# One stream of modulation units through a fourteen-sublayer network on one core: its joins moved into output projections, squares moved from VectorE to ScalarE

## The chip, the cores and the metric

One core of a Trainium2 chip runs the whole program. The metric is the device time of one execution in microseconds (us); the median of several runs is given with the lowest and the highest. One further execution was profiled, and its time stands beside the span that the trace covers. Engines are named as in the profile: PE (TensorE), PEld (its weight loads), DVE (VectorE), ACT (ScalarE), POOL (GpSimd) and SP (SyncE).

## The reference, cut to what matters

Two networks follow each other on the same 256 tokens of width 1024. The first has two layers of three sublayers, the second four layers of two. Each sublayer normalises `x`, scales and shifts it by modulation vectors, computes a mixer or a feed-forward part, and adds the result to `x` through a gate:

```python
mod = (c_act @ mod_w[layer] + mod_b[layer]).reshape(B, N_SUB, 3, D_MODEL)
h, g = sublayer_input(x, norm_g[layer, 0], mod[:, 0])     # rmsnorm(x)*(1+scale)+shift, 1+gate
x = x + MACARON_W * g * swiglu(h, ffn_w_gu[layer, 0], ffn_w_down[layer, 0])
...
mod = c_act @ ada_w[i] + ada_b[i]                          # second network: 6 vectors a layer
h = _rmsnorm(x, norm_g[i, 2]) * (1.0 + sc_f[:, None]) + sh_f[:, None]
y = jnp.square(jax.nn.relu(h @ w1)) @ w2
x = x + gt_f[:, None] * _rmsnorm(y, norm_g[i, 3])
```

The modulation needs a 1024 x 3072 matrix times one vector for each sublayer. It depends on `c` alone, so it can be computed at any time before its sublayer begins.

## The kernel before

The fourteen sublayers, numbered 0 to 13, are ffn1, sb, ffn1, ffn1, lru, ffn1, mla, ffn2, conv, ffn2, pool, ffn2, mla, ffn2. Here ffn1 is the gated feed-forward part, sb the stick-breaking attention, lru the recurrence, mla the second network's attention and ffn2 its squared-ReLU feed-forward part. Products are made in fp32 from a high and a low part of both operands, three matmuls each (L1274 to L1276 with 512 columns, L1375 to L1377 with 256).

**Weights.** SP's queue brings the weights in chunks of 1 MB into `raw` (4 buffers). A chunk is two pieces. For each piece ACT makes `w_hi` (L836) and DVE makes `w_lo` (L1761) in `pieces(a, b)`, and PE uses it in `piece`. There are 4 slots for pieces (`OPS`), so piece p can be made only when PE has used piece p-4. An ffn1 has 11 gate-up jobs of 4 pieces and a down projection of two jobs of 11; an ffn2 has 8 gate-up jobs of 4 pieces and a down projection of two jobs of 16.

**Modulation units.** Each sublayer's modulation is a group of 16 units (`UNITS`). POOL's queue brings a unit's 768 KB into one half of `mod_raw` (`mod_half`, L617 to L621), when the unit two earlier has been used. DVE multiplies it by its entry of `c` and adds it to `mod_acc` (`mod_add`, L1782). Two folds (`mod_fold`, L1788) reduce the accumulator to `mod_t`, PE joins it by 8 small matmuls (`mod_sum`, L1423 to L1428, which waits for both folds), and DVE adds the bias into `mv` (`mod_finish`, L1796). `GROUPS` gives each ffn1 two groups, sb, mla and ffn2 one, until group 13 is given out, so that groups fall on sublayers 0, 1, 2, 3, 5, 6, 7, 9 and 11. The last group of each of these nine is "late": its `mod_sum` is the first thing that PE does in the next sublayer, and its `mod_finish` stands in `a_values`, once the tokens are normalised.

**The boundary of two sublayers.** After the last piece (`last_piece`) DVE multiplies the output by the gate and adds it to `x` (`first_half` and `second_half`, L1882), ACT and DVE normalise, and PE transposes the tokens (`turn_x`, L1319). Where no group is late, PE fills some of this time with small dummy matmuls (`keep_busy`, L1308) before the turn.

**ffn2 gate-up.** ACT makes ReLU into `sig`, DVE squares it into `ev` (L2022), ACT copies it to `hid_hi` and POOL subtracts to `hid_lo` (`hid_low`, L658). Each engine has its own program, in order; semaphores join them.

## Time and profile before

| | before |
|---|---|
| median of 3 runs | 2348.78 us (2347.01 to 2350.11) |
| the profiled execution | 2343.05 us, of which the trace spans 2341.4 us |
| mean granted TensorE clock | 0.958 of full speed |
| PE busy | 2106.8 us (90% of the span) |
| PEld busy | 1906.4 us (81%) |
| DVE busy | 1647.2 us (70%) |
| ACT busy | 1196.4 us (51%) |
| POOL busy | 356.4 us (15%) |
| HBM read | 530.12 MB, 227 GB/s over the span |

All times of the trace are microseconds from the start of its span. Busy shares are means over stages with different limits. A window's PEclk is the share of full TensorE speed that was granted in it; its DMA share is the mean busy share of the core's 16 DMA engines.

### The profile page before, as it was taken

What the parts mean: (1) busy time and instruction counts of PE and PEld (TensorE: products, weight loads), DVE (VectorE), ACT (ScalarE), POOL (GpSimd) and SP (SyncE); (2) the same over time, 40 slices, a digit from 0 to 9 for tenths busy, and PEclk for the clock granted to TensorE, in tenths of its full rate; (3) what the DMA queues carried; (4) which work ended last, traced back from release to release, by engine and by line L of the source; (5) the groups of instructions that cost most, each with busy time, mean ns of one, the idle gap of its engine ahead of it and who ended that gap; (6) DMA issues with size and microseconds to landing.
All of it is one profiled execution on the core that took longest, in us unless ns stands there. A gap on an engine that the chain in (4) does not pass through costs nothing.

```text
span 2341.4 us, 36873 instructions
## 1 busy us (share of the span) xinstructions
PE 2106.8 (90%) x14192; PEld 1906.4 (81%) x14192; DVE 1647.2 (70%) x1861; ACT 1196.4 (51%) x1836; POOL 356.4 (15%) x548
## 2 busy tenths in 40 slices
PE   1999998999899896999887999889997899898998
PEld 1998886998798794998775998758985898777987
DVE  7787865787777867776887776536767776764654
ACT  2553556544554465553565544536544554575543
POOL 2121100111121002121000220430211121000210
PEclk8999999999999997999998999899998899999999
DMA  9798883898888963798666677643777378442653
GB/s 330 259 320 302 281 303 109 284 320 296 269 309 289 284 217 73 257 313 300 212 236 171 222 280 265 180 115 119 266 285 229 103 249 292 143 138 72 196 191 107
DMA packets 298483, 537.72 MB, mean 230 GB/s; under 512 B 11487, under 2 KB 188434, under 8 KB 298352
## 3 DMA queue, kind: packets, MB, share of 16 engines
q1 hardware_dynamic: 262048, 356.55, 46.9%
q0 software_dynamic: 36032, 178.33, 21.8%
q8 instruction: 88, 1.44, 0.2%
q10 hardware_dynamic: 272, 1.05, 0.1%
q14 instruction: 43, 0.35, 0.0%
HBM read 530.12 MB, written 1.11 MB: 227 GB/s over the span
## 4 chain that ended last, share of the span: by engine, by line
PE 73%; DVE 13%; ACT 5%; issue 4%; DMA 3%; POOL 1%; DVEq 0%; ACTq 0%; POOLq 0%
PE bk L1375 12%; PE bk L1377 12%; PE bk L1376 12%; PE bk L1276 7%; PE bk L1275 7%; PE bk L1274 7%; DVE mod_acc L1782 3%; DVE w_lo L1761 3%; DMA mod_raw<-in_ada_w 2%; ACT w_hi L836 2%; PE bk L1262 1%; PE bk L1264 1%; PE bk L1263 1%; PE bk L1319 1%; PE bk L1636 1%
## 5 line engine op out<-in xcount | busy, mean ns | idle before, releaser
L1761 DVE TENSOR_TENSOR w_lo<-raw,w_hi 128x1024 fp32r<-128x1024 f32 (+5 forms) x720 | 832.6, 1185 | 486.7 <-ACT w_hi L836 484.9
L836 ACT ACTIVATE w_hi<-raw 128x1024 fp32r<-128x1024 f32 (+5 forms) x720 | 684.7, 978 | 637.2 <-PE bk L1276 341.9
L1375 PE MATMUL bk<-a_hi,w_hi 128*128 128x256 f32 x2332 | 665.3, 285 | 19.7 <-DVE mv L1799 10.0
L1377 PE MATMUL bk<-a_hi,w_lo 128*128 128x256 f32 x2332 | 663.6, 285 | 0.0
L1376 PE MATMUL bk<-a_lo,w_hi 128*128 128x256 f32 x2332 | 663.5, 285 | 0.0
L1375 PEld LDWEIGHTS bk<-a_hi,w_hi 128*128 128x128 f32 x2332 | 451.5, 194 | 22.3 <-DVE mv L1799 10.8
L1376 PEld LDWEIGHTS bk<-a_lo,w_hi 128*128 128x128 f32 x2332 | 451.5, 194 | 0.0
L1377 PEld LDWEIGHTS bk<-a_hi,w_lo 128*128 128x128 f32 x2332 | 451.4, 194 | 0.0
L1782 DVE SCALAR_TENSOR_TENSOR mod_acc<-mod_raw,cact,mod_acc 128x1536 f32<-128x1536 f32 x182 | 329.8, 1812 | 29.8 <-DMA mod_raw<-in_ada_w 18.3
L1276 PE MATMUL bk<-w_hi,hid_lo 128*128 128x512 f32 x832 | 327.9, 394 | 0.0
L1274 PE MATMUL bk<-w_hi,hid_hi 128*128 128x512 f32 x832 | 324.5, 390 | 3.3 <-DVE w_lo L1761 3.2
L1275 PE MATMUL bk<-w_lo,hid_hi 128*128 128x512 f32 x832 | 326.6, 393 | 0.0
L658 POOL TENSOR_TENSOR hid_lo<-ev,hid_hi 128x512 f32 (+1 forms) x108 | 139.7, 1305 | 546.8 <-ACT hid_hi L1013 440.3
L1274 PEld LDWEIGHTS bk<-w_hi,hid_hi 128*128 128x128 f32 x832 | 156.6, 188 | 39.2 <-issue 4.9
L1275 PEld LDWEIGHTS bk<-w_lo,hid_hi 128*128 128x128 f32 x832 | 156.6, 188 | 35.7
L1276 PEld LDWEIGHTS bk<-w_hi,hid_lo 128*128 128x128 f32 x832 | 156.8, 188 | 31.9
L621 POOL DMA_DIRECT2D mod_raw<-in_ada_w x128 | 69.2, 541 | 632.8 <-DVE mod_acc L1782 518.8
L621 POOL DMA_DIRECT2D mod_raw<-in_mod_w x80 | 43.3, 541 | 432.2 <-DVE mod_acc L1782 323.7
L1319 PE MATMUL bk<-ident,tmp 128*128 128x128 f32 x224 | 47.5, 388 | 60.5 <-DVE tmp L1834 60.2
L1140 ACT ACTIVATE hid_hi<-ev 128x512 f32 (+1 forms) x44 | 27.9, 633 | 139.3 <-DVE ev L2232 139.3
L1274 PE MATMUL bk<-w_hi,a_hi 128*128 128x512 f32 x176 | 71.6, 407 | 28.6 <-POOL a_lo L813 21.7
L1319 PEld LDWEIGHTS bk<-ident,tmp 128*128 128x128 f32 x224 | 39.7, 204 | 66.5 <-DVE tmp L1834 66.3
(361 smaller groups left out, 2997.1 us busy)
## 6 DMA issues: line engine op xcount, KB each, us to landing
raw<-in_ffn_w SPq DMA_DIRECT2D x128, 1024.0 KB, 5.6
mod_raw<-in_ada_w POOLq DMA_DIRECT2D x128, 768.0 KB, 6.2
raw<-in_ffn_w_gu SPq DMA_DIRECT2D x88, 1024.0 KB, 7.4
mod_raw<-in_mod_w POOLq DMA_DIRECT2D x80, 768.0 KB, 6.9
raw<-in_ffn_w_down SPq DMA_DIRECT2D x40, 1024.0 KB, 7.3
first_mod<-in_mod_w SPq DMA_DIRECT2D x16, 768.0 KB, 13.0
raw<-in_sb_w_qkv SPq DMA_DIRECT2D x12, 1024.0 KB, 9.1
raw<-in_conv_w_pw SPq DMA_DIRECT2D x12, 1024.0 KB, 6.2
```

What stands on the lines that cost most here:

```text
L621: pool.dma_start(mod_raw[:, h, :].unsqueeze(1), w.rearrange("(k p) m -> p k m", p=P)[:, bass.ds(r, 1), at + h * MODW:at + (h + 1) * MODW]) ...
L658: pool.tensor_tensor(hid_lo[:, tiles(pair, width), :], ev[:, slot, :, :], hid_hi[:, tiles(pair, width), :].bitcast(F32), ALU.subtract).the ...
L836: ins = act.activation(o(w_hi[:, p % OPS, :]), r(raw[:, c % RAWS, :]), ACT.Copy)
L1274: pe.matmul(o, xh[:, s], wh, start=first, stop=False)
L1275: pe.matmul(o, xh[:, s], wl, start=False, stop=False)
L1276: ins = pe.matmul(o, xl[:, s], wh, start=False, stop=last)
L1319: ins = pe.transpose(turned_x(w, j)[:, P * b:P * b + P], xt[:, b, P * j:P * j + P], ident[:, :])
L1375: pe.matmul(o, wh, a_hi[:, f, :], start=(f == 0), stop=False)
L1376: pe.matmul(o, wh, a_lo[:, f, :], start=False, stop=False)
L1377: ins = pe.matmul(o, wl, a_hi[:, f, :], start=False, stop=(f == KD - 1))
L1761: ins = dve.tensor_tensor(o(w_lo[:, p % OPS, :]), r(raw[:, c % RAWS, :]), o(w_hi[:, p % OPS, :].bitcast(F32)), ALU.subtract)
L1782: dve.scalar_tensor_tensor(out=a, in0=src, scalar=cc[:, bass.ds(r, 1)], in1=a, op0=ALU.mult, op1=ALU.add).then_inc(mod_used, 1)
```

## The change

The units become one stream of 208 that `STREAM` deals to the sublayers: 24, 16, 16, 24, 0, 24, 12, 28, 0, 32, 0, 24, 8, 0. A group may now begin in one sublayer and end in a later one. Sublayers 7 and 9 (ffn2) take 28 and 32 units instead of 16, mla takes 12 and 8 instead of 16 and 0, ffn1 24 or 16 instead of 32. The convolution has none, as before.

`JOINS` names for each sublayer the group joined in the middle and the one joined at its end. In ffn1 the middle join stays in gate-up job 9. The other joins go into `job`, after piece number `at` of an output projection, and their `mod_finish` stands among the pieces there. No join is left at a boundary, so each boundary has `turned()` and `keep_busy`. `mod_sum` writes another bank and its wait for a free bank is left to the caller.

Fold 0 follows the last unit of its group at once; fold 1 (`last_fold`) follows the next piece or pieces. In ffn2's gate-up each job takes two units (before, one), and `DOWN` lists after which pieces of the down projection a unit follows: for 28 units after every second piece, for 32 after two of three. The square of the ReLU goes from DVE (16 in each ffn2) to ACT. DVE's and POOL's loops over jobs of ffn1 and ffn2 are written out.

```diff
-        GROUPS = {"ffn1": 2, "sb": 1, "mla": 1, "ffn2": 1}
-        stages, c, w, hid, grp = [], 0, 0, 0, 1
+        STREAM = (24, 16, 16, 24, 0, 24, 12, 28, 0, 32, 0, 24, 8, 0)
+        JOINS = {0: (1, None), 1: (2, None), 2: (3, None), 3: (4, 5), 5: (6, None), 6: (7, None), 7: (8, 9), 9: (10, 11), 11: (12, None), 12: (13, None)}
+        DOWN = {24: (1, 4, 7, 10, 13, 17, 20, 23), 28: (0, 2, 4, 6, 8, 10, 12, 16, 18, 20, 22, 24), 32: (0, 1, 3, 4, 6, 7, 9, 10, 12, 13, 16, 17, 19, 20, 22, 23)}
...
         for n, kind in enumerate(kinds):
-            groups = list(range(grp, min(grp + GROUPS.get(kind, 0), len(kinds))))
-            late = stages[-1]["groups"][-1] if n and stages[-1]["groups"] else None
-            stages.append(dict(kind=kind, n=n, c=c, w=w, hid=hid, groups=groups, late=late, nth=kinds[:n].count(kind)))
-            c, w, hid, grp = c + CHUNKS[kind], w + WJOBS[kind], hid + PAIRS.get(kind, 0), grp + len(groups)
+            mid, end = JOINS.get(n, (None, None))
+            stages.append(dict(kind=kind, n=n, c=c, w=w, hid=hid, units=STREAM[n], mid=mid, end=end,
+                               nth=kinds[:n].count(kind)))
+            c, w, hid = c + CHUNKS[kind], w + WJOBS[kind], hid + PAIRS.get(kind, 0)
...
         def mod_out(w):
-            return bk[:, 4 * (w % 2) + 1, S:S + MODC // P]
+            return bk[:, 4 * (w % 2) + 3, 0:MODC // P]
...
+            def loads(n):
+                for _ in range(n):
+                    s = k.next("load")
+                    if s < NSTREAM:
+                        mod_half(1 + s // UNITS, s % UNITS // 2, s % 2)
...
                 if st["kind"] == "ffn2":
-                    g, n = st["groups"], st["hid"]
-                    def two_low(i, b):
+                    n = st["hid"]
+                    for j in range(8):
+                        loads(min(2, st["units"]))
                         for e in range(2):
-                            hid_low(n + 4 * i + 2 * b + e, 4 * i + 2 * b + e, e)
-                    with pool.Fori(0, 4) as i:
-                        for b in range(2):
-                            two_low(i, b)
-                            if g and b == 1:
-                                mod_load(g[0], i + 1)
+                            hid_low(n + 2 * j + e, 2 * j + e, e)
                     gate_tile(st["n"])
-                    if g:
-                        for r in range(5, KD):
-                            mod_next(g[0], r)
-                    if g:
-                        mod_next(g[0], KD)
+                    loads(max(0, st["units"] - UNITS))
...
                 elif st["kind"] == "ffn1":
-                    g, n = st["groups"][0], st["hid"]
-                    mod_rest(g, lambda i, b: hid_low(n + 2 * i + b, 2 * i + b, b))
-                    for b in range(3):
-                        if b:
-                            mod_next(g + 1, b)
-                        hid_low(n + 8 + b, 8 + b, b % 2)
+                    n, more = st["hid"], st["units"] > UNITS
+                    for b in range(11):
+                        loads(2 if b < 8 else more)
+                        hid_low(n + b, b, b % 2)
                     gate_tile(st["n"])
...
+                    n, s0 = st["hid"], 16 * st["nth"]
                     with act.Fori(0, 4) as i:
                         for b in range(2):
                             pieces(p + 4 + 4 * b, p + 8 + 4 * b, i)
                             for e in range(2):
                                 relu(w + b, c + 2 * b, i, e)
                             for e in range(2):
-                                if e:
-                                    is_read(act, w + b, i)
-                                else:
-                                    act.wait_ge(prod_ready, 8 * st["nth"] + 2 * i + b + 1)
+                                act.wait_ge(sig_ready, n + 2 * b + e + 1 + 4 * i)
+                                act.wait_ge(hid_ready, n + 2 * b + e + 1 + 4 * i)
+                                act.activation(ev[:, e, :, :], sig[:, e, :, :], ACT.Square).then_inc(prod_ready, 1)
+                            act.sem_inc(bank_free[(w + b) % 2], 1)
+                            for e in range(2):
+                                act.wait_ge(prod_ready, s0 + 2 * b + e + 1 + 4 * i)
                                 act.activation(hid_hi[:, tiles(4 * i + 2 * b + e), :], ev[:, e, :, :], ACT.Copy)\
                                     .then_inc(hhi_ready, 1)
...
-            def job(c, w, i, xs, kt0, kts, ready, outs=None, tail=None):
+            def job(c, w, i, xs, kt0, kts, ready, outs=None, tail=None, join=None, at=None):
                 is_free(pe, w, i)
                 n = (kts + 1) // 2
                 for q in range(n if tail is None else n - 1):
                     piece(2 * c + q, i, ready, xs, kt0 + 2 * q, outs or by_feature(w), q == 0, q == n - 1)
+                    if join is not None and q == at:
+                        mod_sum(join, w)
...
             def mod_sum(g, w):
-                is_free(pe, w)
                 pe.wait_ge(mod_folded, 2 * (g + 1))
...
-                if st["late"]:
-                    mod_sum(st["late"], w)
-                elif g:
+                if g:
                     is_free(pe, w)
+                    turned()
                     keep_busy(job_banks(w)[:, 3, :], 16 if after(g) == "post" else 6)
-                if g:
                     turn_x(w)
-                turned()
...
-                    job(c + 16, w + 8, 0, H, 0, F2 // P, lambda f: (hid_ready, 2 + st["hid"] + f // 2 + 1), by_token(w + 8))
-                    job(c + 24, w + 9, 0, H, 0, F2 // P, None, by_token(w + 9), tail=True)
+                    job(c + 16, w + 8, 0, H, 0, F2 // P, lambda f: (hid_ready, 2 + st["hid"] + f // 2 + 1), by_token(w + 8),
+                        join=st["mid"], at=3)
+                    job(c + 24, w + 9, 0, H, 0, F2 // P, None, by_token(w + 9), tail=True, join=st["end"], at=10)
...
-                    job(c + 10, w + 10, 0, A, 0, KD, None, by_token(w + 10))
+                    job(c + 10, w + 10, 0, A, 0, KD, None, by_token(w + 10), join=st["mid"], at=1)
...
-                        gate_up(c + 2 * b, w + b, 0, second=(lambda: mod_sum(st["groups"][0], w + 10)) if b == 9 else None)
+                        def sums():
+                            is_free(pe, w + 10)
+                            mod_sum(st["mid"], w + 10)
+                        gate_up(c + 2 * b, w + b, 0, second=sums if b == 9 else None)
...
-                    job(c + 28, w + 12, 0, H, 0, 22, None, by_token(w + 12), tail=True)
+                    job(c + 28, w + 12, 0, H, 0, 22, None, by_token(w + 12), tail=True, join=st["end"], at=6)
...
+            def unit():
+                s = k.next("unit")
+                g, u = 1 + s // UNITS, s % UNITS
+                mod_add(g, u // 2, u % 2)
+                if u == UNITS - 1:
+                    mod_fold(g, 0)
+            def last_fold():
+                s = k.get("unit")
+                if s and s % UNITS == 0 and k.get("folds") < s // UNITS:
+                    k.add("folds", 1)
+                    mod_fold(s // UNITS, 1)
...
-                if stages[g]["late"]:
-                    mod_finish(stages[g]["late"], w)
...
                 if st["kind"] == "ffn2":
                     n = st["hid"]
-                    def two_jobs(i):
-                        for b in range(2):
-                            pieces(p + 4 + 4 * b, p + 8 + 4 * b, i)
-                            if st["groups"]:
-                                mod_add(st["groups"][0], i, b)
-                            for e in range(2):
-                                dve.wait_ge(sig_ready, n + 2 * b + e + 1 + 4 * i)
-                                dve.wait_ge(hid_ready, n + 2 * b + e + 1 + 4 * i)
-                                dve.tensor_tensor(ev[:, e, :, :], sig[:, e, :, :], sig[:, e, :, :], ALU.mult)\
-                                    .then_inc(bank_free[(w + b) % 2] if e else prod_ready, 1)
-                    two_jobs(0)
-                    with dve.Fori(1, 4) as i:
-                        two_jobs(i)
-                    for u in range(8):
-                        pieces(p + 36 + 4 * u, p + 39 + 4 * u - u // 7)
-                        if st["groups"]:
-                            mod_add(st["groups"][0], 4 + u // 2, u % 2)
-                            if u >= 6:
-                                mod_fold(st["groups"][0], u - 6)
-                        if u == 3:
+                    units = st["units"]
+                    for j in range(8):
+                        for h in range(2):
+                            pieces(p + 4 + 4 * j + 2 * h, p + 6 + 4 * j + 2 * h)
+                            if units:
+                                last_fold()
+                                unit()
+                    for q in range(31):
+                        if q == 4 and st["mid"]:
+                            mod_finish(st["mid"], w + 8)
+                        if q == 15:
                             first_half(g, w + 8, c + 24)
-                        if u < 7:
-                            pieces(p + 39 + 4 * u, p + 40 + 4 * u)
-                    pieces(p + 66, p + 67)
+                        if q == 27 and st["end"]:
+                            mod_finish(st["end"], w + 9)
+                        pieces(p + 36 + q, p + 37 + q)
+                        last_fold()
+                        if q in DOWN.get(units, ()):
+                            unit()
                     second_half(g, w + 9, c + 32)
...
-                            if m in (2, 3, 5, 6):
-                                unit(6 + (2, 3, 5, 6).index(m))
-                    for j in range(3):
-                        unit(10 + j)
-                        pieces(p + 24 + j, p + 25 + j)
+                            last_fold()
+                            if m in (2, 3, 4, 5, 6, 7)[:max(0, units - 6)]:
+                                unit()
+                    pieces(p + 24, p + 26)
+                    if st["mid"]:
+                        mod_finish(st["mid"], w + 10)
+                    pieces(p + 26, p + 27)
                     first_half(g, w + 10, c + 12)
-                    unit(13)
-                    pieces(p + 27, p + 28)
-                    unit(14)
-                    pieces(p + 28, p + 29)
-                    unit(15)
-                    pieces(p + 29, p + 31)
+                    pieces(p + 27, p + 31)
...
+                    more = st["units"] > UNITS
+                    for b in range(11):
+                        for h in range(2):
+                            pieces(p + 4 + 4 * b + 2 * h, p + 6 + 4 * b + 2 * h)
+                            last_fold()
+                            if b < 8:
+                                unit()
                         if b == 9:
-                            mod_finish(st["groups"][0], w + 10)
-                        mod_add(st["groups"][1], b - 8, 0)
+                            mod_finish(st["mid"], w + 10)
+                        if b >= 8 and more:
+                            unit()
                         product(w + b, c + 2 * b + 2, b % 2, n + b)
                     for m in range(2):
                         for u in range(6 - m):
                             pieces(p + 48 + 12 * m + 2 * u, p + 50 + 12 * m + 2 * u)
-                            if u < 6 - 2 * m:
-                                v = 5 + 7 * m + u + (m == 0 and u > 2)
-                                mod_add(st["groups"][1], v // 2, v % 2)
-                                if v >= 14:
-                                    mod_fold(st["groups"][1], v - 14)
-                            if m == 0 and u == 2:
-                                mod_add(st["groups"][1], 4, 0)
+                            last_fold()
+                            if more and u in ((0, 2, 4), (0, 1))[m]:
+                                unit()
                         if m:
+                            if st["end"]:
+                                mod_finish(st["end"], w + 12)
                             second_half(g, w + 12, c + 34)
                         else:
                             first_half(g, w + 11, c + 28)
...
                             if m < 6:
-                                mod_add(st["groups"][0], 5 + m // 2, m % 2)
-                                if m >= 4:
-                                    mod_fold(st["groups"][0], m - 4)
-                    pieces(p + 28, p + 31)
+                                unit()
```

## Rows read from the trace of the kernel before

**Rows 1.** Page: chain of work that ended last, by engine.

```profile
PE 73%; DVE 13%; ACT 5%; issue 4%; DMA 3%; POOL 1%; DVEq 0%; ACTq 0%; POOLq 0%
```

**Rows 2.** Windows at boundaries: length, PE busy (matmuls), PEclk, DMA share, GB/s.

```profile
257.32:266.15 8.83, 3.91 (x26) 0.81 0.97 228
400.54:406.09 5.55, 2.57 (x26) 1.00 0.64 204
599.14:608.72 9.58, 3.99 (x26) 0.74 1.11 221
934.25:939.91 5.66, 4.07 (x30) 1.00 1.10 352
1269.33:1283.79 14.46, 4.29 (x26) 0.62 0.87 160
2143.41:2153.38 9.97, 7.42 (x50) 0.83 0.22 77
```

**Rows 3.** Timeline of DVE, end of sublayer 0: start, duration, work.

```profile
253.75 1.82 DVE L1782 SCALAR_TENSOR_TENSOR mod_acc<-mod_raw,cact,mod_acc 128x1536 f32<-128x1536 f32 x1
255.60 1.78 DVE L1788 TRANSPOSE_TENSOR_REDUCE mod_t<-mod_acc 128x48 f32<-128x1536 f32 x1
...
259.54 0.68 DVE L1882 TENSOR_TENSOR tmp<-bk,sig 128x512 f32<-128x512 f32 x1
```

**Rows 4.** Timeline of DVE, end of sublayer 4.

```profile
934.17 0.68 DVE L1882 TENSOR_TENSOR tmp<-bk,sig 128x512 f32<-128x512 f32 x1
```

**Rows 5.** Windows: length; PE, PEld, DVE, ACT, POOL busy (instructions); PEclk, DMA share, GB/s.

```profile
742.76:803.25 60.49, 60.45 (x266) 49.32 (x264) 48.64 (x38) 25.93 (x30) 7.78 (x14) 1.00 0.86 312
1076.15:1140.47 64.32, 62.03 (x265) 50.49 (x264) 52.03 (x45) 25.77 (x34) 8.71 (x15) 0.97 0.89 319
1283.79:1377.04 93.25, 93.25 (x769) 93.25 (x768) 68.48 (x65) 51.86 (x71) 21.14 (x20) 0.99 0.67 226
1703.91:1791.57 87.66, 87.66 (x385) 71.93 (x384) 59.12 (x47) 38.83 (x43) 8.38 (x13) 1.00 0.82 282
2245.91:2333.57 87.66, 87.66 (x386) 71.93 (x384) 39.08 (x34) 36.69 (x43) 3.09 (x3) 1.00 0.44 146
```

**Rows 6.** DMA issues in 540:600, 1078:1138 and 1703:1792: count, KB, median us to landing.

```profile
mod_raw<-in_mod_w POOLq DMA_DIRECT2D x10, 768.0 KB, 7.0
...
mod_raw<-in_ada_w POOLq DMA_DIRECT2D x12, 768.0 KB, 6.4
...
mod_raw<-in_ada_w POOLq DMA_DIRECT2D x10, 768.0 KB, 4.8
```

**Rows 7.** Window of ten us in sublayer 0, columns as in rows 5.

```profile
210.00:220.00 10.00, 10.00 (x45) 8.23 (x44) 6.53 (x6) 3.19 (x3) 1.06 (x2) 1.00 1.04 405
```

**Rows 8.** Timeline of ACT and DVE in sublayer 7, one piece.

```profile
1459.76 1.06 ACT L836 ACTIVATE w_hi<-raw 128x1024 fp32r<-128x1024 f32 x1 [1.68 <-PE bk L1276]
...
1460.85 1.23 DVE L1761 TENSOR_TENSOR w_lo<-raw,w_hi 128x1024 fp32r<-128x1024 f32 x1 [1.23 <-ACT w_hi L836]
```

**Rows 9.** Windows of mla 6 and 12: before the heads' loop, then the loop.

```profile
1163.48:1206.14 42.66, 38.96 (x282) 36.43 (x281) 33.93 (x53) 29.40 (x56) 3.20 (x6) 0.96 0.63 228
2040.03:2081.54 41.51, 38.98 (x282) 36.60 (x281) 26.42 (x48) 29.23 (x56) 0.00 (x0) 0.96 0.44 139
1206.14:1247.65 41.51, 31.83 (x195) 21.33 (x193) 33.20 (x82) 24.79 (x83) 2.65 (x5) 0.96 0.51 173
2081.54:2121.74 40.20, 31.61 (x194) 20.96 (x192) 25.32 (x76) 24.95 (x84) 1.45 (x2) 0.96 0.22 72
```

**Rows 10.** Timeline of PE: a join in gate-up of sublayer 0.

```profile
174.87 0.28 PE L1428 MATMUL bk<-mod_t,stripes 128*32 128x24 f32 x8
```

**Rows 11.** Window behind the wait at the join of sublayer 2, columns as in rows 5.

```profile
525.20:528.60 3.40, 3.40 (x18) 3.40 (x18) 2.16 (x2) 0.63 (x1) 0.50 (x1) 0.50 0.88 282
```

**Rows 12.** Page, groups: busy, mean ns of one; idle before them, releaser.

```profile
L1375 PE MATMUL bk<-a_hi,w_hi 128*128 128x256 f32 x2332 | 665.3, 285 | 19.7 <-DVE mv L1799 10.0
...
L658 POOL TENSOR_TENSOR hid_lo<-ev,hid_hi 128x512 f32 (+1 forms) x108 | 139.7, 1305 | 546.8 <-ACT hid_hi L1013 440.3
...
L2022 DVE TENSOR_TENSOR ev<-sig 128x512 f32<-128x512 f32 x64 | 41.2, 685 | 0.0
```

124 lines of the change are left out of this document (47 added, 77 removed).

## The prediction, on record before the changed kernel ran

> **What bounds the kernel now.** I read the chain of waits first: 73% of it is PE's own work and 13% DVE's [rows 1]. PE is the bound inside the large stages, so the change can win only where PE waits: at boundaries, and where a piece or a join comes late. Next come windows over the boundaries, each from PE's last weight matmul to its first one in the next sublayer [rows 2]. 0 to 1 takes 8.83 us, 2 to 3 9.58, mla 6 to its ffn2 14.46. Two rows are the yardsticks: lru's boundary, without a late join, takes 5.66, and mla 12's, also without one, 9.97. But the sb sublayer's boundary has a late join and takes 5.55 [rows 2]: a late join whose folds were done early costs nothing. The reader is to see that lateness of DVE, not the join, makes these boundaries long. The timeline shows it: at the end of sublayer 0 DVE adds a unit at 253.75, folds at 255.60, and starts the gate's product only at 259.54, 2.28 us after PE's end at 257.32 [rows 2, 3]; at the end of lru it starts at 934.17, before PE's end at 934.25 [rows 2, 4]. Then windows over whole projections give PE's pace, 87.66 us for 32 pieces of 12 matmuls in an ffn2's down projection, so 2.74 us a piece, and the same 87.66 with half a group of units and its folds beside it as with none [rows 5]. Last, the DMA issues say how fast a unit lands [rows 6].
>
> **Gains.** The ffn1 sublayers now end with no unit after DVE's last pieces but two, so I take their boundaries to lru's length: 8.83 - 5.66 = 3.2 for 0 to 1, 9.58 - 5.66 = 3.9 for 2 to 3, and 3.9 for 3 to 4, which shows the same pattern as 2 to 3. mla 6 loses six units and two folds from its output projection: 14.46 - 9.97 = 4.5 [rows 2]. Together 15.5. ffn1 sublayer 5 takes 64.32 us for its down projection where sublayer 3 takes 60.49 [rows 5]; with five units there in place of eleven I take it to 60.49, gain 3.8. The folds that leave the sb heads' loop: two of 1.78 us [rows 3], between nothing and 3.5; DVE is mostly hidden there, so 0.5.
>
> The clock: a stall at the ffn1 join, 10.0 us in four sublayers [rows 12], is followed by 3.40 us at PEclk 0.50 [rows 11], so by 1.7 us lost. The late boundaries show PEclk 0.62 to 0.81, the lru one 1.00 [rows 2]. If the four shortened ones and sublayer 5 gave back 1.7 each it would be 8.5; if shorter idle doesn't change the grant, nothing. With what the other late boundaries give I take the middle, 4. Gains: 15.5 + 3.8 + 0.5 + 4 = 23.8.
>
> **Costs.** *Joins inside projections.* Nine sums move from a boundary where PE idles into a PE that is full. One takes 0.28 us as a block of eight [rows 10], so 0.3 each, 2.7.
>
> *Where such a join waits for its folds,* PE stands. A piece needs 1.06 us on ACT and 1.23 on DVE, 2.32 from the release to the end and some 2.4 with the release itself [rows 8]; a unit takes 1.8 and a fold 1.8 [rows 3]. With four slots, piece p begins when p-4 has been used. Sublayer 3: after piece 59 DVE makes 63 (2.4), a unit 1.8, fold 0 1.8, two pieces 2.4, fold 1 1.8: 10.2 us; PE reaches the join after three pieces, 8.2. Stall 1.9 with its semaphore, less what the unit's place saves: I take 1.7. Sublayer 7: the last unit follows piece 60, so 2.4 + 1.8 + 1.8 + 1.2 + 1.8 = 9.0 after piece 56; PE arrives after two pieces, 5.5. Stall 3.3 to 3.5, taken 3.3. Sublayer 9: the same chain begins one piece earlier, so PE has 8.2 us for 8.8: 0.6, if DVE is on time. A stall lowers the clock as above; in proportion to rows 11 and 12 (2.5 us stalled, 1.7 lost, and not more) that adds 1.0 and 1.7. So 2.7 and 5.0.
>
> *Is DVE on time in sublayer 9?* Two units now follow every three pieces, 8.2 us of PE. The two halves of `mod_raw` refill only when used, so a pair needs a transfer, an add and its issue: 6.4 to 7.0 [rows 6] + 1.8 [rows 3] + 0.3 = 8.5 to 9.1 us. That is 0.3 to 0.9 too long; over seven pairs 2 to 6, middle 4.2. The first of these loads stands on POOL behind the last two `hid_low` of 1.3 us [rows 12], which adds up to 2.6, taken 2.0. The longer gap after the eighth unit gives back a piece of 2.74, less two gated products of 0.68 [rows 3] and the adds to x, some 1.9 when the pairs are resumed late. Lag 4.3, stall 4.9, and 1.7 of clock: 6.6. The slack before pieces themselves are late is about 5.5 us (four pieces, 11.0, less 2.4 for the making and 2.74 for the one in use), so I charge nothing more. Bounds: 0.6, and 15 if the lag passes the slack and each pair then stalls.
>
> *mla.* The heads' loop of mla 6 takes 41.51 with four units, that of mla 12 40.20 with none [rows 9]: 1.3 us for 7.3 us of DVE. After, six units and two folds stand in it, 7.2 us more: 1.3 by this ratio, 7.2 if nothing hides them; near the ratio, 2.0. mla 12 gets six units ahead of the loop (42.66 - 41.51 = 1.15 [rows 9]) and two units and two folds in it, 7.2 us on DVE: 1.3 by the ratio, up to 7.2. I take 1.2 + 2.3 = 3.5.
>
> *Hidden.* The squares: 16 in an ffn2, each 0.685 us on DVE [rows 12]. ACT's Square isn't in these rows at this shape; between a copy's length of zero and that of a `w_hi`, 1.06 [rows 8], it adds 0 to 17 us to ACT's 51.86 of 93.25 [rows 5], so ACT stays under 69. DVE loses 11 and gets eight more units in sublayers 7 and 9, 14.5: 68.48 becomes 72. PE is full all through this window, so I take nothing; if a square delays a piece there, PE would show idle time in gate-up. Two units a job make 16 chunks and 16 units in 93.25 us: 16.8 + 12.6 MB, 315 GB/s, which sublayer 5's projection already carries at 319 [rows 5]. The unrolled loops remove branches and add instructions to fetch: nothing of either is in PE's path by rows 1, taken as zero. `keep_busy` takes the idle that the join left, zero.
>
> Costs: 2.7 + 2.7 + 5.0 + 6.6 + 2.0 + 3.5 = 22.5.
>
> **The sum.** 23.8 - 22.5 = 1.3 gained, against the profiled execution of 2343.05: 2341.75. That execution lies 5.73 under the median of 2348.78, so 2347.5 for the median of runs. A difference of 0.2%, 4.7 us, is about what a measurement of this kernel can tell from none; so forecast: no change.
>
> **A page beside it.** Whether units of sublayer 9 land in time hangs on what the transfers can reach; a window in sublayer 0 shows 405 GB/s over ten us [rows 7]. The Trainium skill, "Perfetto Trace Analysis", section Engine Utilization (Roofline), gives 358 GB/s of HBM for a core when both of a pair are active, and says that a core alone can pull more, up to its 16 DMA engines at about 435. The row of 405 agrees with the second. By 358 the 3.15 MB of three pieces and two units would take 8.8 us, an estimate that leaves the sum as it is; by 435 they would take 7.2 and the lag of sublayer 9 would fall away, which is the next case.
>
> **Rivals.** *Faster, 2339.* The unit's transfer in an ffn2's down projection lands in 4.8 us today [rows 6]. If it still does with two units per three pieces, a pair needs 6.9 us of 8.2, the lag is gone and sublayer 9 costs 0.6 instead of 6.6 (6.0 back). mla then goes by the ratio too, since only late units held it (1.9 back): 2347.5 - 7.9 = 2339.6. For it: rows 6 and 7. Against: 4.8 was measured at 282 GB/s [rows 5], and with 319 and more in flight units took 6.4 to 7.0.
>
> *Slower, 2354.* Three pieces bring 1.5 MB of weights and two units 1.5, 3.15 MB in 8.2 us, 383 GB/s. If the queues hold only the 319 to 325 that whole projections show [rows 5], that takes 9.8 us, 1.5 over, and eight times it is 12 us of PE, with pieces themselves late, instead of the lag's 4.9: 2347.5 + 7 = 2354.5. It decides from the point at which pair and weights together need over 8.9 us. For it: no projection window here is above 319. Against: the ten us at 405.
>
> *The boundaries don't shrink, 2357.* Their chain of DVE, ACT, DVE sets the length, and taking DVE's late units away only moves the idle elsewhere: half of the 19.5 of boundaries and clock stays away, +10. For it: sb's row has 5.55 with a join. Against: the 2.28 us of lateness in rows 3.
>
> **How the numbers follow.** The forecast has 0.42, the faster case 0.33, the slower 0.19, the boundaries 0.06. The forecast is within 4.7 us of before, so that is the chance of no change; slower is 0.19 + 0.06 = 0.25. The range takes the faster case with the 3 us that the clock may give more, 2336, and the slower one with the upper bound of the mla terms, 2358; the forecast's own is 2343 to 2352.
>
> **What would show it.** Right: PE's boundary windows after 0, 2 and 3 at 5.5 to 6.5 us with PEclk near 1; mla 6's at 10; idle of PE before the sum at the end of sublayers 3, 7 and 9, of 1.7, 3.3 and 5 us; ffn2's gate-up at 93.25 with PE full. Wrong: idle of PE before w_lo in gate-up of 7 or 9 (squares or transfers late), a stall in sublayer 9 under 1 us (faster case) or idle before pieces all through its down projection (slower case), boundaries of ffn1 still at 8 us or more.

## The result, and the profile after

The changed kernel takes 2355.91 us (median of 11 runs, 2349.24 to 2361.0); the kernel before takes 2347.31 in the same series (11 runs, 2340.19 to 2351.87). The ratio is 1.0037, 95% interval 1.0024 to 1.0051: slower by 8.6 us where I had forecast 1.3 us faster and called it no change. It landed near the slower rival's time, 2354, but not for that rival's reason. The profiled execution of after took 2361.0, the highest of its 11, and that of before 2343.05, 4.3 under its median, so the two traces are 17.6 us of span apart and about half of that is by chance of the two executions.

PE's share of the chain of waits is what it was [rows 1]:

```profile
PE 73%; DVE 13%; ACT 6%; issue 4%; DMA 3%; POOL 1%; DVEq 0%; ACTq 0%; SPq 0%; POOLq 0%
```

The boundaries of after (windows: length, PE busy, PEclk, DMA share, GB/s), behind sublayers 0, 2, 3 and 6:

```profile
257.15:262.93 5.78, 4.15 (x31) 1.00 0.58 182
602.74:608.40 5.66, 4.06 (x30) 1.00 0.57 185
808.19:814.60 6.41, 4.54 (x31) 0.87 0.76 196
...
1273.55:1283.54 9.99, 6.99 (x50) 0.85 0.63 198
```

The boundary of before behind sublayer 3, which [rows 2] leave out:

```profile
803.25:813.44 10.19, 4.00 (x27) 0.76 1.04 180
```

Against this and [rows 2] the four are 3.05, 3.92, 3.78 and 4.47 us shorter, 15.2 where the forecast had 15.5. The timeline of DVE at the end of sublayer 0 says why: the last piece at 255.93, the gate's product at 257.07, 0.08 us before 257.15 and not 2.28 after 257.32 [rows 3]. What the forecast calls PE's end is in both the start of PE's last weight matmul, which takes 0.39 us more; and of the 2.28 us of before a part goes to two more pieces that DVE makes between the fold and the product.

```profile
255.93 1.23 DVE L1731 TENSOR_TENSOR w_lo<-raw,w_hi 128x1024 fp32r<-128x1024 f32 x1 [1.52 <-ACT w_hi L798]
257.07 0.69 DVE L1865 TENSOR_TENSOR tmp<-bk,sig 128x512 f32<-128x512 f32 x1
```

So the gain came. What took it back is in the windows over whole stages (columns as in rows 5). In order: the down projections of sublayers 3 and 5, gate-up and down of 7, down of 9, the heads' loop of mla 6, the heads' loop and output projection of mla 12:

```profile
744.05:808.19 64.14, 62.27 (x274) 50.63 (x272) 41.71 (x35) 26.02 (x30) 5.04 (x8) 0.97 0.64 221
1077.57:1137.78 60.21, 60.21 (x266) 49.40 (x264) 38.45 (x37) 25.77 (x34) 5.57 (x9) 1.00 0.75 255
1283.54:1376.03 92.49, 92.49 (x770) 92.48 (x769) 81.76 (x61) 58.66 (x85) 33.38 (x28) 1.00 0.84 290
1376.03:1469.33 93.30, 90.17 (x401) 73.24 (x400) 69.15 (x56) 39.77 (x45) 10.53 (x17) 0.98 0.88 308
...
1705.94:1800.59 94.65, 90.55 (x401) 73.10 (x400) 76.91 (x63) 39.78 (x45) 12.64 (x21) 0.98 0.94 335
...
1202.77:1249.90 47.13, 36.18 (x193) 23.75 (x193) 38.70 (x85) 23.73 (x82) 3.73 (x7) 0.85 0.54 176
...
2090.94:2137.29 46.35, 35.80 (x195) 23.66 (x193) 32.94 (x81) 24.87 (x83) 0.53 (x1) 0.85 0.24 84
2137.29:2161.00 23.71, 23.71 (x103) 19.22 (x104) 10.09 (x12) 10.27 (x14) 0.91 (x1) 0.93 0.22 50
```

The down projection of sublayer 5 gains 4.1 us and gate-up of 7 stays full of PE. The three projections with an end join lose 3.65, 5.64 and 6.99 us, the two loops 5.62 and 6.15 against [rows 5, 9].

The join itself can be read in the timeline of sublayer 7. DVE's rows show the last unit, fold 0, one piece, fold 1, one behind the other; PE's row shows the join waiting for the last of them:

```profile
1447.56 1.81 DVE L1752 SCALAR_TENSOR_TENSOR mod_acc<-mod_raw,cact,mod_acc 128x1536 f32<-128x1536 f32 x1
1449.29 1.77 DVE L1758 TRANSPOSE_TENSOR_REDUCE mod_t<-mod_acc 128x48 f32<-128x1536 f32 x1
1450.98 1.18 DVE L1731 TENSOR_TENSOR w_lo<-raw,w_hi 128x1024 fp32r<-128x1024 f32 x1
1452.09 1.77 DVE L1758 TRANSPOSE_TENSOR_REDUCE mod_t<-mod_acc 128x48 f32<-128x1536 f32 x1
...
1453.91 0.28 PE L1394 MATMUL bk<-mod_t,stripes 128*32 128x24 f32 x8 [3.13 <-DVE mod_t L1758]
```

The waits of PE in the down projections of 3, 7 and 9, and of DVE in that of 9 (us in total, times, longest):

```profile
PE bk L1394 <- DVE mod_t L1758: 1.9, 1, 1.9
...
PE bk L1394 <- DVE mod_t L1758: 3.1, 1, 3.1
...
PE bk L1394 <- DVE mod_t L1758: 4.0, 1, 4.0
...
DVE mod_acc L1752 <- DMA mod_raw<-in_ada_w: 9.6, 9, 1.9
```

I had put these stalls at 1.7, 3.3 and 4.9 us. In sublayer 9 DVE waits nine times for a unit to land, 9.6 us in all, as the forecast's lag said.

### The profile page after: what moved, and what is told of

Read it like the earlier page. It is cut to its first block, busy times and chain, and to the rows that moved or that the text cites. A ratio compares the mean times of both kernels' runs of the same rounds, so it can differ in the third digit from the quotient of the medians.

```text
span 2359.0 us, 36511 instructions
## 1 busy us (share of the span) xinstructions
PE 2141.5 (91%) x14380; PEld 1934.8 (82%) x14380; DVE 1625.9 (69%) x1797; ACT 1224.9 (52%) x1900; POOL 371.8 (16%) x548
## 4 chain that ended last, share of the span: by engine, by line
PE 73%; DVE 13%; ACT 6%; issue 4%; DMA 3%; POOL 1%; DVEq 0%; ACTq 0%; SPq 0%; POOLq 0%
PE bk L1342 11%; PE bk L1343 11%; PE bk L1344 11%; PE bk L1239 8%; PE bk L1241 8%; PE bk L1240 8%; DVE w_lo L1731 3%; DVE mod_acc L1752 3%; DMA mod_raw<-in_ada_w 2%; ACT w_hi L798 2%; PE bk L1227 1%; PE bk L1229 1%; PE bk L1228 1%; PE bk L1601 1%; PE bk L1319 1%
## 5 line engine op out<-in xcount | busy, mean ns | idle before, releaser
L1731 DVE TENSOR_TENSOR w_lo<-raw,w_hi 128x1024 fp32r<-128x1024 f32 (+5 forms) x720 | 847.3, 1202 | 534.1 <-ACT w_hi L798 531.8
L1342 PE MATMUL bk<-a_hi,w_hi 128*128 128x256 f32 x2332 | 666.6, 286 | 22.1 <-DVE mv L1784 10.0
L1343 PE MATMUL bk<-a_lo,w_hi 128*128 128x256 f32 x2332 | 664.6, 285 | 0.0
L1752 DVE SCALAR_TENSOR_TENSOR mod_acc<-mod_raw,cact,mod_acc 128x1536 f32<-128x1536 f32 x182 | 335.9, 1846 | 20.1 <-DMA mod_raw<-in_ada_w 19.0
L637 POOL TENSOR_TENSOR hid_lo<-ev,hid_hi 128x512 fp32r<-128x512 f32 x108 | 153.8, 1434 | 165.4 <-ACT hid_hi L978 100.3
L1227 PE MATMUL bk<-a_hi,w_hi 128*128 128x256 f32 x280 | 79.5, 284 | 1.7 <-DVE a_lo L1839 1.2
L1228 PE MATMUL bk<-a_lo,w_hi 128*128 128x256 f32 x280 | 79.2, 283 | 0.0
```

The source lines that it names most:

```text
L637: pool.tensor_tensor(hid_lo[:, tiles(pair, width), :], ev[:, slot, :, :], hid_hi[:, tiles(pair, width), :].bitcast(F32), ALU.subtract).the ...
L1227: pe.matmul(o, wh[:, s], xh, start=first, stop=False)
L1342: pe.matmul(o, wh, a_hi[:, f, :], start=(f == 0), stop=False)
L1343: pe.matmul(o, wh, a_lo[:, f, :], start=False, stop=False)
L1731: ins = dve.tensor_tensor(o(w_lo[:, p % OPS, :]), r(raw[:, c % RAWS, :]), o(w_hi[:, p % OPS, :].bitcast(F32)), ALU.subtract)
L1752: dve.scalar_tensor_tensor(out=a, in0=src, scalar=cc[:, r:r + 1], in1=a, op0=ALU.mult, op1=ALU.add).then_inc(mod_used, 1)
```

## The experiments

The edits are to the changed kernel if nothing else is said. Ratios are to the kernel before, with 95% intervals.

**e1, the end joins later.**

```diff
-  join=st["end"], at=10)      # ffn2
+  join=st["end"], at=13)
-  join=st["end"], at=6)       # ffn1
+  join=st["end"], at=8)
-  if q == 27 and st["end"]:
-      mod_finish(st["end"], w + 9)
   ...
+  if st["end"]:
+      mod_finish(st["end"], w + 9)
   second_half(g, w + 9, c + 32)
```

> The end joins go later: behind piece 8 in place of 6 in ffn1 sublayer 3, behind piece 13 in place of 10 in ffn2 sublayers 7 and 9, and their mod_finish behind DVE's last piece. If PE stood there because DVE's chain (last unit, fold, piece, fold) was not done, the stalls of 2.3, 3.5 and 4.4 us and the half clock behind them go: the down projections fall from 64.1, 93.3 and 94.7 us to about 60.5, 88 and 88 to 90, and the whole is 12 to 16 us under the changed kernel, ratio to before 0.997 to 1.000. Rival, transfers of units in sublayer 9 come late whatever the join: its projection stays above 91 us, with waits for w_lo in place of the join's, and only 8 us or less come back. Rival, the joins' own matmuls or mod_finish cost the time: no change.

2337.62 us, 0.9974 (0.9961 to 0.9986): 1.0037 - 0.9974 is 0.0063, 14.8 us under the changed kernel, and a little faster than before. The windows of the three projections:

```profile
739.29:799.91 60.62, 60.62 (x274) 49.47 (x272) 41.69 (x35) 26.00 (x30) 5.04 (x8) 1.00 0.66 234
1366.13:1454.64 88.51, 88.51 (x401) 72.10 (x400) 68.66 (x54) 39.76 (x45) 10.53 (x17) 1.00 0.93 327
1691.43:1780.43 89.00, 89.00 (x401) 71.80 (x400) 76.21 (x61) 39.77 (x45) 12.66 (x21) 1.00 0.98 356
```

PE is busy from end to end in all three, at 1.00, and 3.52 + 4.79 + 5.65 = 14.0 us are back. Sublayer 9 carries the same units at 356 GB/s with a DMA share of 0.98; their lag is still there (DVE waits 9.9 us for them) but in this trace nothing of PE waits for it. So the long stalls were the place of the join and not the transfers. The lag does reach PE in part in e7, e9 and e10, which have this very stage: it takes 90.22, 89.51 and 90.50 us there, and PE waits 1.0, 0.3 and 0.9 us for a piece. In e10:

```profile
PE bk L1239 <- DVE w_lo L1731: 0.9, 1, 0.9
...
DVE mod_acc L1752 <- DMA mod_raw<-in_ada_w: 11.0, 10, 2.9
```

With 30 units in place of 32 (e6, e8, e11) the projection takes 88.51 us. The two joins that are left in sublayer 7 cost 88.51 - 87.66 = 0.85 us, 0.42 each where I had 0.3.

**e2, no adds in the mla loops.** In both heads' loops DVE's adds and folds of units are left out (their transfers and semaphores stay), so the modulation vectors of groups 7, 8 and 13 lack them.

```diff
-  last_fold()
-  if m in (2, 3, 4, 5, 6, 7)[:max(0, units - 6)]:
-      unit()
+  if k.get("unit") % UNITS == 0 and k.get("folds") < k.get("unit") // UNITS:
+      k.add("folds", 1)
+      ...
+      dve.sem_inc(mod_folded, 1)
+  if m in (2, 3, 4, 5, 6, 7)[:max(0, units - 6)]:
+      ...
+      dve.sem_inc(mod_used, 1)
```

> In the heads' loops of both mla sublayers DVE leaves out the adds and folds of the units (6 units and 2 folds, 2 units and 2 folds); the transfers and every count stay, so the modulation vectors of groups 7, 8 and 13 are not the reference's. If DVE's work in the loop is on PE's path, the loops fall from 47.1 and 46.4 us to 40 to 41.5, the projections behind them from 23.7 to 21.7 as the clock stays up, 14 to 16 us in all, ratio to before about 0.997. Rival, it is the transfers of the units or the clock by itself: the loops stay above 45 us and the ratio at 1.003. Rival in between, only the adds beyond the four of before count: 5 to 8 us.

2345.69 us, 1.0005 (0.9992 to 1.0018), so 0.0032 or 7.5 us under the changed kernel. The two loops:

```profile
1195.85:1237.65 41.80, 34.43 (x195) 22.80 (x193) 26.43 (x77) 24.88 (x83) 3.82 (x7) 0.88 0.62 205
2079.79:2121.74 41.95, 34.30 (x194) 22.71 (x193) 26.57 (x77) 24.89 (x83) 0.53 (x1) 0.88 0.29 94
```

ACT's waits in the loop of mla 6, in after and in e2, say how DVE's work reaches PE, which waits for ACT there (7.9 us in after, 4.9 in e2):

```profile
ACT mp L1045 <- DVE low L2088: 16.0, 7, 3.8
...
ACT mp L1045 <- DVE low L2088: 9.9, 7, 2.5
```

The loops fall as expected if DVE's work is on PE's path, and the transfers, which stayed, are cleared. The total came back by half of what I expected and lies in the range of the rival in between, 5 to 8. The loops of after stand near the upper end of their spread: over the traces that hold the same loops (after, e1, e3, e7, e9, e10) the means are 44.7 and 45.4, and against these e2 falls by 2.9 and 3.4.

**e3, the squares back on DVE.**

```diff
   # ACT: the two Squares and their sem_inc go; Copy waits for DVE as before
   # DVE, after the two units of each job:
+  for e in range(2):
+      ...
+      dve.tensor_tensor(ev[:, e, :, :], sig[:, e, :, :], sig[:, e, :, :], ALU.mult)\
+          .then_inc(bank_free[(w + j) % 2] if e else prod_ready, 1)
```

> The squares of ffn2 go back to DVE, as in the kernel before; all else as changed. If the move was hidden, the four gate-up windows stay at 92.5 to 93.4 us with PE full and the time within 3 us of the changed kernel, ratio 1.002 to 1.005. Rival, the move is what made room for two units a job: gate-up of sublayers 7 and 9 grows by more than 1 us each, or the end of their down projection comes later by 2 us each, ratio above 1.005. Rival, ACT's squares delay the pieces: the time falls by 3 us or more.

2376.84 us, 1.0139 (1.012 to 1.0158): 24 us over the changed kernel by the ratios (4 runs). The windows of gate-up of 7 and down of 9, and two rows of waits in that gate-up:

```profile
1273.75:1372.64 98.89, 94.18 (x771) 92.64 (x769) 80.64 (x73) 51.16 (x72) 25.60 (x28) 1.00 0.78 266
...
1709.13:1808.02 98.89, 91.77 (x399) 74.47 (x400) 80.07 (x66) 38.34 (x43) 12.61 (x21) 0.97 0.90 327
...
PE bk L1340 <- DVE w_lo L1729: 4.4, 6, 1.8
...
ACT hid_hi L976 <- DVE ev L2005: 41.3, 7, 7.4
```

ACT's copy of the square waits 41.3 us for DVE, whose square stands behind two units; ACT makes no `w_hi` in that time, and PE waits for pieces. The denser stream would have been a large loss without this part. The rival, "the move is what made room for two units a job", is the one that holds.

**e5, the squares alone in the kernel before.** The same Squares on ACT, with before's stream and joins.

> The kernel before with one part of the change alone: the squares of ffn2 on ACT. If the move only makes room on DVE for the denser stream, PE stays full in gate-up and the ratio to before is 0.998 to 1.002; if it saves by itself, under 0.997. The profile is also a second look at stages that this edit does not touch: sb's heads, 41.1 us from the first score to the output projection in the one trace of before and 43.7 to 44 in the five of the changed kind. If that difference is made by the change, it is 41 here again with no half clock in it; if it is chance of the clock grant, it is 43 or more. The same for ffn1 gate-up of sublayer 3, 134.0 against 135.5 us.

2343.87 us, 1.0003 (0.9991 to 1.0014): worth nothing with one unit a job. In stages that its edit leaves alone its trace is a second sample of before, and it corrected my yardsticks. The heads of sb, then the loops of mla 6 and 12:

```profile
337.65:379.48 41.83, 34.07 (x240) 26.72 (x240) 24.33 (x25) 29.53 (x41) 4.07 (x7) 0.96 0.44 141
...
1203.61:1250.71 47.10, 37.02 (x194) 24.09 (x192) 33.35 (x82) 24.85 (x83) 2.63 (x5) 0.82 0.45 151
...
2080.21:2122.32 42.11, 34.42 (x194) 22.84 (x192) 25.40 (x76) 25.02 (x84) 1.44 (x2) 0.88 0.26 69
```

The same instructions of mla 6 that took 41.51 at 0.96 in [rows 9] take 47.10 at 0.82 here. The heads of sb stay near before's 41.12 us at 1.00, with some half clock (PEclk 0.50, the lower of its two levels) in them.

**e4, joins late, mla's units earlier.** `STREAM` (24, 16, 24, 24, 0, 24, 6, 28, 0, 32, 0, 24, 6, 0), with end joins in 2, 5, 7 and 9.

> End joins as in the first kernel of this call, and eight units go to sublayer 2 (16 to 24), taken from mla 6 (12 to 6) and mla 12 (8 to 6), so that no unit stands in a heads' loop; groups then end in sublayers 2, 5, 7 and 9, and sublayer 5 has an end join too. If both causes are right they add: 22 to 30 us under the changed kernel, ratio to before 0.990 to 0.994. If only the joins count: 0.997 to 1.000. Rival, units in sublayer 2's projection bring its boundary back to 9 us and its gain is spent: ratio 0.995 or more.

2337.93 us, 0.9966 (0.9955 to 0.9978), about e1's: 16.7 us under the changed kernel by the ratios where I had expected 22 to 30. The loop of mla 6, with nothing in it, took 40.85 us, but that of mla 12, with one fold left at its start, 44.82, nearly the 45.4 of the loops with two units and two folds; and sublayer 9's projection, with 32 units, took 91.59, with PE waiting 2.2 us in it for pieces.

**e6, units in the convolution.** Joins late; (24, 16, 20, 24, 0, 24, 6, 28, 8, 30, 0, 24, 4, 0), no unit and no fold in a heads' loop.

> End joins late as in e1, and units dealt anew: 24, 16, 20, 24, 0, 24, 6, 28, 8, 30, 0, 24, 4, 0. Eight stand in the convolution, mla keeps 6 and 4, all ahead of the heads' loop, folds too. If DVE's work in the mla loops is the second cause, the loops go to 40 to 42 us and the projections to 21.7 in both, 8 to 10 us under e1, ratio to before 0.992 to 0.995, provided that the convolution hides eight adds. Rival, the convolution does not hide them: its 124 to 126 us grow by 5 us or more (8 adds are 14.5 us) and the ratio stays at 0.997. Rival, the loops stay at 44 us with no unit in them, so the clock alone sets them: 0.997 too.

2345.06 us, 1.0008 (0.9997 to 1.0018). I had expected 0.992 to 0.995. The loops were 41.55 and 40.46, but the convolution of e6 takes 135.36 us,

```profile
1461.64:1597.00 135.36, 110.29 (x1035) 91.90 (x1034) 74.36 (x91) 53.21 (x83) 40.74 (x75) 0.91 0.61 168
```

against 123.92 in after: eight adds of 14.5 us cost 11.4, with PE's own work unchanged at 110 us. The change's "none in the convolution" is right.

**e8, units ahead of the heads.** Joins late; (24, 16, 24, 24, 0, 24, 6, 30, 0, 30, 0, 26, 4, 0), the last fold before the loop.

> End joins late as in e1; units 24, 16, 24, 24, 0, 24, 6, 30, 0, 30, 0, 26, 4, 0: none in the convolution, none and no fold in either heads' loop, 30 in sublayers 7 and 9. In e4 the loop of mla 12 still held one fold and took 44.8 us, that of mla 6 held nothing and took 40.9. If a fold or add in the loop is the cause, both loops take 40 to 42 here and both projections 21.7 to 22.1, 5 us under e4 and 6 to 9 under e1, ratio to before 0.993 to 0.996. Rival, chance of the clock grant sets the loops: one of them is above 44 again. Rival, 24 units in sublayer 2 and its end join give it all back: 0.997.

2332.67 us, 0.9940 (0.9927 to 0.9954), inside what I expected. Both loops are about as short as the shortest without a unit, 40.20 [rows 9]:

```profile
1199.69:1240.31 40.62, 32.68 (x194) 21.54 (x193) 26.43 (x77) 24.84 (x83) 1.43 (x2) 0.92 0.42 97
2071.29:2111.76 40.47, 31.62 (x195) 20.96 (x193) 24.62 (x76) 24.74 (x83) 0.53 (x1) 0.96 0.22 72
```

The projection behind mla 12 stayed at 23.73 us with half clock in it, where I had expected 21.7 to 22.1.

**e7, e9, e10, PE's idle filled.** All on e1. e7 puts 20 dummies ahead of sb's heads; e9 puts 10 there, and 12 and 26 at boundaries for 6 and 16; e10 puts 20 for 6 at the first boundary alone.

```diff
+  keep_busy(job_banks(w + 5)[:, 3, :], 20)
   is_read(pe, w + 4)
```

> e1 with 20 small dummy matmuls of PE, about 2.2 us, in the 2.5 us in which it waits ahead of sb's first head. They write a bank that nobody reads; the output stays the reference's. If idle PE is what brings the half clock at the start of sb's heads, which costs the 2.6 us by which sb is longer than before, the heads take 41.1 us again in place of 43.7 and the total falls by 2 to 3 us against e1. Rival, the half clock follows something else: 43.7 us again, the same time as e1 within 1.5 us.

> e1 with PE's idle filled: keep_busy with 12 dummies in place of 6 at boundaries of the plain kind and 26 in place of 16 at the others (0.23 us each, so 1.4 and 2.3 us of the 1.8 and 2.7 us idle behind them), and 10 ahead of sb's heads, 2.3 of 2.5 us idle (20 of them took 4.6 us and put the first head off by 2 us). Output as the reference. If idle of PE at these places is what brings half clock in the stage behind, half clock at the start of sublayers 2, 3, 5 and 6 and at sb's heads goes, sb falls from 134.6 to 132 and the whole by 3 to 6 us under e1. Rival, half clock there follows idle inside the stages, which stays: the same time as e1 within 2 us, sb at 134 to 135.

> e1 with 20 dummies in place of 6 at the first boundary alone: 14 more of 0.23 us, 3.2 us, against 1.8 us of idle behind them, so the boundary grows from 5.78 to about 7.2 us and PE is busy in all of it. If the change's gain at that boundary is given back in sb because half clock falls on the beginning of its heads, moving sb by 1.4 us can move the half clock off them: sb at 132 to 133 in place of 134.6 and the sum of boundary and sb no longer than e1's 140.4. Rival, sb is slower for a reason inside it: 134.6 again and the sum 141.8.

Windows of sb run here from its first to its last weight matmul, 134.39 us before and 137.09 in e1; the expectations count it 2.5 us shorter. e7: 2343.17, 0.9993 (0.9981 to 1.0006). Its dummies were sized wrong, 4.6 us for 2.5 us of idle, and sb grew to 142.65; it tells nothing of the clock. e9: 2338.09, 0.9973 (0.9961 to 0.9986), the same as e1 and not the 3 to 6 us that I had expected, although its trace has 133 us at half clock in all where e1's has 164. e10: 2342.39, 0.9985 (0.997 to 1.0); boundary and sb together 144.6 us against e1's 142.9, so the longer boundary gained nothing. The heads of sb in after, and in e9:

```profile
334.49:378.23 43.74, 36.55 (x240) 28.56 (x240) 21.00 (x23) 29.31 (x41) 3.17 (x6) 0.88 0.43 138
```

```profile
333.85:374.61 40.76, 32.55 (x242) 25.60 (x241) 20.95 (x23) 29.24 (x41) 3.17 (x6) 1.00 0.46 145
```

With full clock the heads take 40.76 in the changed order too, so the excess in after is the clock's. But e9 shows half clock in the output projection behind instead (23.73 us where e1 has 22.11), and sb as a whole takes 136.11, still 1.7 over before.

**e11, the join in gate-up moved too.** e8 with the middle join of ffn1 behind piece 2 of its down projection.

```diff
-  gate_up(c + 2 * b, w + b, 0, second=sums if b == 9 else None)
+  gate_up(c + 2 * b, w + b, 0)
   ...
-  job(c + 22, w + 11, 0, H, 0, 22, ..., by_token(w + 11))
+  job(c + 22, w + 11, 0, H, 0, 22, ..., by_token(w + 11), join=st["mid"], at=2)
   ...
+  if m == 0 and u == 1:
+      mod_finish(st["mid"], w + 11)
```

> e8 with the one join that the change left in gate-up taken out too: the middle join of the five... of each ffn1 sublayer (0, 2, 3, 5) goes behind piece 2 of its down projection, its mod_finish among DVE's pieces there. In every trace so far PE stands 2.78 us at gate-up job 9 in each of the four, for DVE's mv, and half clock follows for 3.4 us in most. If nothing takes the wait's place, gate-up of 0, 2, 3 and 5 falls from 133.5, 134.1, 135.3 and 135.7 by 2.8 to 4.5 us each, 11 to 18 us in all, ratio to before 0.986 to 0.990. Rival, DVE is late in the down projection instead and PE waits there: 5 us or less come back, ratio 0.992 or more.

2320.16 us, 0.9884 (0.9864 to 0.9903), the best of all, 27 us under before. PE's wait in gate-up of sublayer 0 in e8, and the same gate-up in e11:

```profile
PE bk L1342 <- DVE mv L1784: 2.5, 1, 2.5
```

```profile
63.11:191.39 128.28, 128.28 (x1057) 128.09 (x1057) 95.03 (x86) 67.95 (x79) 22.87 (x28) 1.00 0.88 296
```

Gate-up of 0, 2, 3 and 5 falls by 5.2, 4.7, 4.0 and 4.7 us against e8, more than the 2.5 of the wait, since the half clock behind it, and in sublayer 0 that at the start, goes as well. No wait of the join's took its place. Of these 18.6 us the medians show 12.5. In the two traces 3.4 went to the lru sublayer (122.70 and 126.11 us), which lies between 120.7 and 125.1 in the other traces.

## Why the prediction was wrong

The table sets the forecast's terms against the profiled pair, and against means over traces: for stages as before the traces of before and e5; for stages as changed those of after, e1, e2, e3, e7, e9 and e10, each where it did not edit the stage. Windows of the same stage, in us. The forecast's 17.0 has all nine sums in it; in the measured columns three of them stand in the rows of sb and mla.

| term | forecast | the pair | means |
|---|---|---|---|
| boundaries behind 0, 2, 3, 6 | -15.5 | -15.2 | -14.2 |
| down of sublayer 5 | -3.8 | -4.1 | -3.3 |
| clock and other boundaries, folds out of sb | -4.5 | +6.4 | +2.9 |
| ffn joins, with stalls and lag | +17.0 | +16.7 | +16.9 |
| mla 6 | +2.0 | +6.9 | -0.1 |
| mla 12 | +3.5 | +9.3 | +6.3 |
| sum | -1.3 | +20.0 | +8.5 |

The means add up to what the medians show, 8.6; that they do so this closely is luck, as each rests on two to seven traces. The pair's sum is over its 17.6 since the convolution, 2.6 us shorter by chance, is not in it. The row of the clock and sb is worked out, in the means, as sb +2.5, gate-up of 2 and of 3 together +3.7, the downs of 0 and 2 -1.4, and the other boundaries -1.9. Not all of it is the clock.

**Right.** The boundaries: DVE's lateness set them, and its going gave what the forecast said. The joins' stalls: the chain unit, fold, piece, fold against PE's pieces, 1.7, 3.3 and 4.9 us forecast and 1.9, 3.1 and 4.0 measured; e1 shows it by moving the join. The lag in sublayer 9 from units that land late: 9.6 us of DVE's waits; the slack before pieces held in after and e1, and fell short by 0.3 to 1.0 us in e7, e9 and e10. Squares hidden on ACT: e5 finds them worth nothing alone. The slower rival's mechanism, transfers that hold up PE's pieces, is not what cost the time: PE waits for no piece in sublayer 9 of after, and the same bytes go through in 89.00 to 90.50 us with the join late, at 356 GB/s in e1 and not at the rival's 319 to 325. That the rival's number was close is luck. The Trainium skill, "Perfetto Trace Analysis", section Engine Utilization (Roofline), lets a core alone pull more than 358 GB/s; the stage mean of 356 stays below that figure and the trace shows more only in short stretches, as in [rows 7].

**The step that failed: "The clock", 4 us to be given back, with 0.5 from sb.** I took half clock at a late boundary as a loss that goes with the boundary. It did go from there (PEclk 1.00 in 5.66 us behind sublayer 2 against 0.74 [rows 2]), but where PE idles at a boundary half clock costs little (behind sublayer 3 it is 6.41 us at 0.87 in after and 6.13 at 1.00 in e1), and it turned up in stages where PE works. In sb's heads it was 1.00 before, 0.96 in e5, 0.92 in e1 and 0.88 in after, for 41.12, 41.83, 43.37 and 43.74 us. Of sb's 2.5 us the join in its projection takes 0.4. In gate-up of sublayer 3 the wait at the join is the same 2.5 us before, after and in e1. Before and in e5 half clock stands in the first 1.8 and 2.0 us of the stage alone; in the traces of the changed kind 3.4 us of it stand behind the join, or 6.8 near the start, and the stage is 1.6 us longer. The balance of the row is a loss of 2.9 where I had a gain of 4.5. What a wait inside gate-up and the clock behind it cost together e11 shows by taking the wait away.

One part of the row is not the clock and had no term in the sum. In gate-up of sublayer 2 PE waits for pieces, 2.5 us in after and 1.4 to 1.6 in the other traces of the changed kind, and not at all before or in e5. In after:

```profile
PE bk L1342 <- DVE w_lo L1731: 2.5, 2, 2.0
```

The longest of these waits comes behind the last unit of group 3 and its fold 0, which DVE now has ahead of that job's product; in sublayer 3 a group ends at the same place without such a wait, so the cause is not shown.

Why half clock falls on sb's heads in this order of the work the runs do not show: dummies ahead of the heads only moved it into the projection behind, and a longer first boundary didn't remove it. The two traces of before may also be lucky ones there.

**Mis-sized: mla 12, "1.3 by the ratio", taken as 2.3.** The ratio rested on 41.51 against 40.20 [rows 9], and e5 shows the first to be a good draw: the same instructions took 47.10. Loops without a unit keep to 40.2 to 42.1 us in eleven windows of seven traces; with units they lie between 41.5 and 47.1. So the 7.2 us of adds and folds cost mla 12 some 4.2 us, not 1.3 to 2.3; one fold alone cost as much in the one trace of e4, so the price does not seem to go by DVE's busy time. The projection behind, its join included, is 1.5 longer, but as long in e6, e8 and e11 with nothing in the loop, so this is not the adds'. mla 6 had the swing already, and in the means the change added nothing there. Also small: a join costs 0.42 in place of 0.3.

With the clock and sb at nothing the forecast's own terms give -15.5 - 3.8 + 17.0 + 2.0 + 3.5 = +3.2, and with mla 12 at its measured 6.3, +6.0: slower. The joins were costed at 14.3 us with stalls, and e1 shows that a later `at` alone would have turned the result round; the prediction named the chain and did not ask what the change would be worth without it.

## What to carry to other kernels

When a reduction's last step moves into a busy engine's stream, count the producers' chain from the last input to the point of use in units of that engine's work, and place the use behind it: two or three pieces of 2.74 us were worth 14 us here. Work "hidden" in a loop that is bound by waits has to be priced from several executions, since one window can be a lucky draw by more than the whole effect. An idle gap that is closed may only move the low clock to a place where it costs more, so a gain in clock is not to be booked before a trace shows it; take away the waits inside full stages first.

## What the runs showed of the hardware

The spread of a stage whose instructions are the same: the heads' loop of mla 6 at 41.51 us and PEclk 0.96 in before and 47.10 and 0.82 in e5. The runs do not show what decides it.

POOL and DVE hold each other up when they overlap. With squares on DVE, half of POOL's `hid_lo` run beside a piece of DVE's and the others beside nothing; with squares on ACT they run beside DVE's pieces and adds. Groups of after, then of e3, both in gate-up of sublayer 7 (busy, mean ns):

```profile
L637 POOL TENSOR_TENSOR hid_lo<-ev,hid_hi 128x512 fp32r<-128x512 f32 x14 | 25.8, 1856 | 0.1
...
L1752 DVE SCALAR_TENSOR_TENSOR mod_acc<-mod_raw,cact,mod_acc 128x1536 f32<-128x1536 f32 x13 | 28.1, 2160 | 2.6 <-DMA mod_raw<-in_ada_w 2.6
```

```profile
L637 POOL TENSOR_TENSOR hid_lo<-ev,hid_hi 128x512 fp32r<-128x512 f32 x14 | 17.9, 1293 | 6.1 <-ACT hid_hi L976 6.1
...
L1750 DVE SCALAR_TENSOR_TENSOR mod_acc<-mod_raw,cact,mod_acc 128x1536 f32<-128x1536 f32 x12 | 21.7, 1806 | 0.0
```

`hid_lo` takes 1856 ns for 1293 and an add 2160 for 1806. Inside the trace of after the adds with no `hid_lo` beside them take 1.80 to 1.82 us, and those with one 2.18 to 2.86. It is the one that starts second that is longer: in e3 `hid_lo` starts first and keeps its 1.3 us, and the piece behind it takes 2.13 to 2.16 us where one alone takes 1.21. DVE is busy 81.76 us in gate-up of 7 where I had worked out 72: the longer adds, 4.6, and two folds that the forecast left out, 3.5, are most of the difference. PE did not wait for any of it in after.

The Trainium skill, "SBUF — State Buffer", section Who interferes with whom, says that a VectorE instruction with two inputs in SBUF and a GpSimd instruction that reads SBUF contend for a shared port pair, which is an exclusive lock, and that the order of issue decides who blocks. The spans agree with it, though those on POOL are rough.
